# Shift added as rows: a two-block kernel's first k, v and queries projected from h without adaLN's shift

## The chip, the cores and the metric

One core of a Trainium2 chip runs the whole program. The metric is device time in microseconds (us) for one execution, the median of several runs; less is better. Everything is float32.

## What is computed

The input is x (256 tokens by 2048) and a context ctx of the same size. A first block of two layers (adaLN, one input projection, attention with pooling and Fourier branches, gates, an output projection) is followed by a second block (spatial gating, an LRU and an FFN). The change touches the first layer of the first block only:

```python
shift, scale, gate = jnp.split(jax.nn.silu(c) @ ada_w[l] + ada_b[l], 3, axis=-1)
h = rmsnorm(x, norm_g[l]) * (1.0 + scale[:, None]) + shift[:, None]
hc = rmsnorm(xc, norm_g[l]) * (1.0 + scale_c) + shift_c        # the context, with c_ctx
qc, kc, vc, upc, ufc, gc = split_proj(hc @ w_in[l])
q, k, v, up, uf, g = split_proj(h @ w_in[l])                   # 1024, 256, 256, 512, 512, 2048 columns
q = apply_axial_rope(rmsnorm(q.reshape(B, N, N_HEADS, HEAD_DIM), q_norm_g[l]), cos, sin)
k = apply_axial_rope(rmsnorm(k.reshape(B, N, N_KV_HEADS, HEAD_DIM), k_norm_g[l]), cos, sin)
att = latent_attention(q, k, v, kc, vc)
x_new = x + gate[:, None] * (jnp.concatenate([att, pool, fourier], -1) * silu(g)) @ w_out[l]
```

Here silu(c) @ ada_w[l] needs 2048 by 6144 weights (50 MB) for two vectors, the one of x and the one of the context.

## The kernel before

**Chunks.** All large weights come through one ring: the list `chunks` holds one entry per 512 KB of a weight matrix, SyncE loads them in order into RAW (NRAW = 8 buffers, `load_ahead`, L257, and L1071). A load is put once the chunk eight places before it is released: a chunk of the ada form when it is multiplied, another when it is split. There are two kinds of work on a chunk:
- ada chunks (256 rows of ada_w by 512 columns): TensorE (PE) multiplies them in plain float32 against the two vectors silu(c), silu(c_ctx) (L1104), 8 chunks to one of 12 groups of 512 columns per layer: groups 0 to 3 are the shift, 4 to 7 the scale, 8 to 11 the gate. Then ACT copies the sums out (`ada_out`, L1330), PE turns them (L1172), and DVE writes them as columns (L1576 to L1584); the last two steps are a popped step, `spread`.
- the others are split into two fp32r parts, high on ACT (L1320), low on DVE (L1546), in one of NSPL = 4 buffers, and multiplied three times. In layer 0 tokens and context go together ("wide": 24 matmuls of 128x512 per chunk). k and v (the `kv` group), q0 (heads 0 to 3), q1 (heads 4 to 7), the pool input gp, the Fourier input gf and the eight gate groups use L1123 to L1125 or L1137 to L1139. The output projection out0 has 8 groups of 4 chunks.

**One list sets the order.** The program is written once as a list `order` of steps; every engine runs its own instructions of each step in that order, waiting on semaphores. `run_chunks` (L307) goes through the chunks: `run_ahead` (L272) first puts the splits of the next chunks (those up to START_AHEAD = 3 places on while the position is under 72, AHEAD = 5 later), then small steps are popped from two queues, `hi` and, if that is empty, `low` (`pop_side`, L286: in layer 0 one step per half chunk; in the start two per two ada chunks), then the matmuls are put, then what the chunk triggers (`then`). `need` pops further steps until the h that a chunk reads has been put.

**The start of layer 0** (`start`, L707): for u = 0 to 3 eight ada chunks of scale group 4+u and eight of shift group u; from u = 1 on two kv chunks between them, after 12 and after 16 ada chunks; then the last two kv chunks. In `hi` stand the squares of x, the 16 turns of x into columns (`turn_x`, L1158 on PE, L1557 on DVE) and rstd (L979). The end of each u appends eight tiles of h (`tile_h`, L433: DVE L1590, ACT L1338, DVE L1595), and for u = 3 the loads of the rope tables, `tables` (L475, DVE L1606 and L1609, waits for the spill of x) and the DFT load. x is spilled from XT to memory (L1936), since XT is used again for QS, the rows of q, k and v.

**After it** come q0, q1, gp, gf and the gates, with two chunks of `left` (16 later ada groups, 128 chunks) after every two (`mixed`, L344), then out0 in the same manner (L942), eight ada chunks (FILL), and layer 1. At the end of a projection `rows_out` (L485; ACT L1356, DVE L1617) copies PSUM banks to QS; `norm_item` (L497) squares, scales, ropes and turns. Attention goes in units of one head and 128 queries; `unit_row` (L555) runs four stages of four units, scores (PE L1187), max, exp (ACT L1383), scaling, turns (L1194) and the product with v (L1204). There are 32 units in layer 0, heads 0 to 3 first in the list; `gate_out` (L644) of heads j0 and j0+1 pops until their units are put (the gate groups come in the order 8, 10, 0, 2, 4, 6, 12, 14). `x_out` (L692) at the end of an out0 group adds to x (DVE L1714) and puts two squares (ACT L1454).

## Time and profile before

| | |
|---|---|
| median of 3 runs | 2459.34 us (2458.92 to 2460.93) |
| the profiled execution | 2455.74 us, of which the profile's span is 2453.9 us |
| mean granted TensorE clock in it | 0.976 |
| PE busy | 2318.9 us, 94% |
| DVE, ACT, POOL busy | 1288.8, 1044.1, 196.6 us |
| memory read and written | 428.37 and 6.29 MB, 177 GB/s |

The engines are PE (TensorE), DVE (VectorE), ACT (ScalarE), POOL (GpSimd) and SP (SyncE). A matmul's record is longer than its spacing, since matmuls are pipelined, so costs of PE are read from starts. Where an engine stood idle, the profile says what ended the wait. Idle time of an engine that does not set the end costs nothing.

### The profile page before, as it was taken

The numbers are of one execution on the slowest core, as the hardware profiler recorded it, in microseconds if no ns is written. First come the engines' busy times: TensorE is split into PE (matmuls) and PEld (weight loads), VectorE is DVE, ScalarE is ACT, GpSimd is POOL, SyncE is SP. The second block draws the span as 40 slices with busy tenths as digits, with TensorE's granted clock in tenths as the row PEclk, the third lists the DMA queues.
The fourth block names the chain that finished last, engine by engine and source line by source line (L and its number), as shares of the span: only waits on it lengthen the run. The fifth ranks groups of instructions, "written<-read, shape, count | busy, mean of one in ns | idle before, by whom it ended". The sixth has DMA issues, their size and how long they took to land.

```text
span 2453.9 us, 30582 instructions
## 1 busy us (share of the span) xinstructions
PE 2318.9 (94%) x12135; PEld 1857.9 (76%) x12135; DVE 1288.8 (53%) x2110; ACT 1044.1 (43%) x1596; POOL 196.6 (8%) x237
## 2 busy tenths in 40 slices
PE   5889999999999997899998988989999999999998
PEld 2467777777777665678887877868888888888887
DVE  2444533132332254445666786556765666566664
ACT  2232333342321263445544555445543555345543
POOL 1000100000010122100012014120000000000001
PEclk8989999999999998999999999989999999999999
DMA  9764343435655583534555554545555555566652
GB/s 367 284 246 163 131 140 108 138 104 172 240 172 172 183 302 114 188 105 141 186 172 155 175 186 129 173 135 187 184 189 185 184 186 187 190 188 188 195 187 89
DMA packets 347021, 436.66 MB, mean 178 GB/s; under 512 B 13848, under 2 KB 269280, under 8 KB 345984
## 3 DMA queue, kind: packets, MB, share of 16 engines
q1 hardware_dynamic: 341376, 413.19, 51.1%
q0 software_dynamic: 3408, 16.38, 1.8%
q10 hardware_dynamic: 2096, 5.15, 0.6%
q8 instruction: 96, 1.57, 0.3%
q14 instruction: 45, 0.37, 0.0%
HBM read 428.37 MB, written 6.29 MB: 177 GB/s over the span
## 4 chain that ended last, share of the span: by engine, by line
PE 84%; DVE 5%; ACT 4%; DMA 3%; POOL 2%; issue 2%; SPq 0%; ACTq 0%; POOLq 0%; DVEq 0%
PE ps L1142 31%; PE ps L1143 16%; PE ps L1137 5%; PE ps L1139 5%; PE ps L1138 5%; PE ps L1123 4%; PE ps L1125 4%; PE ps L1124 4%; PE ps L1104 3%; ACT SPL L1320 2%; DMA RAW<-in_w_in_dram 2%; DVE SPL L1546 1%; PE ps L1187 1%; PE ps L1204 1%; DMA RAW<-in_ada_w_dram 1%
## 5 line engine op out<-in xcount | busy, mean ns | idle before, releaser
L1142 PE MATMUL ps<-HS,SPL 128*128 128x512 f32 x3456 | 1230.0, 401 | 18.0 <-POOL HS L1998 17.0
L1546 DVE TENSOR_TENSOR SPL<-RAW,SPL 128x1024 fp32r<-128x1024 f32 x592 | 725.7, 1231 | 667.2 <-ACT SPL L1320 665.6
L1143 PE MATMUL ps<-HS,SPL 128*128 128x256 f32 x3456 | 968.8, 280 | 0.0
L1320 ACT ACTIVATE SPL<-RAW 128x1024 fp32r<-128x1024 f32 x592 | 621.8, 1057 | 538.1 <-PE ps L1143 349.6
L1142 PEld LDWEIGHTS ps<-HS,SPL 128*128 128x128 f32 x3456 | 654.3, 189 | 182.3 <-POOL HS L1998 17.6
L1143 PEld LDWEIGHTS ps<-HS,SPL 128*128 128x128 f32 x3456 | 656.6, 190 | 2.1 <-issue 1.9
L1123 PE MATMUL ps<-SPL,HS 128*128 128x512 f32 x576 | 248.0, 430 | 22.3 <-ACT XT L1362 8.6
L1125 PE MATMUL ps<-SPL,HS 128*128 128x512 f32 x576 | 228.3, 396 | 0.0
L1124 PE MATMUL ps<-SPL,HS 128*128 128x512 f32 x576 | 228.1, 396 | 0.0
L1137 PE MATMUL ps<-HS,SPL 128*128 128x512 f32 x512 | 212.3, 415 | 1.2 <-DVE HS L1702 1.2
L1139 PE MATMUL ps<-HS,SPL 128*128 128x512 f32 x512 | 200.5, 392 | 0.0
L1138 PE MATMUL ps<-HS,SPL 128*128 128x512 f32 x512 | 200.1, 391 | 0.0
L1123 PEld LDWEIGHTS ps<-SPL,HS 128*128 128x128 f32 x576 | 110.5, 192 | 72.8 <-issue 20.8
L1993 POOL TENSOR_TENSOR TMP<-TMP 128x256 f32<-128x256 f32 (+1 forms) x68 | 61.6, 906 | 1235.2 <-ACT TMP L1454 1232.7
L1124 PEld LDWEIGHTS ps<-SPL,HS 128*128 128x128 f32 x576 | 110.6, 192 | 26.7 <-issue 6.0
L1137 PEld LDWEIGHTS ps<-HS,SPL 128*128 128x128 f32 x512 | 96.6, 189 | 43.8 <-issue 16.1
L1125 PEld LDWEIGHTS ps<-SPL,HS 128*128 128x128 f32 x576 | 110.1, 191 | 24.8
L1104 PE MATMUL ps<-RAW,CW 128*32 128x512 f32 x768 | 114.5, 631 | 11.4 <-DMA RAW<-in_ada_w_dram 9.3
L1454 ACT ACTIVATE TMP<-XT 128x256 f32<-128x256 f32 (+1 forms) x72 | 33.5, 465 | 191.9 <-DVE XT L1714 124.1
L1138 PEld LDWEIGHTS ps<-HS,SPL 128*128 128x128 f32 x512 | 96.7, 189 | 22.4 <-issue 3.8
L1139 PEld LDWEIGHTS ps<-HS,SPL 128*128 128x128 f32 x512 | 96.4, 188 | 21.1
L1899 DVE SCALAR_TENSOR_TENSOR MM<-MM,VV 128x256 f32<-128x256 f32 x192 | 80.0, 478 | 0.0
(251 smaller groups left out, 1542.0 us busy)
## 6 DMA issues: line engine op xcount, KB each, us to landing
RAW<-in_w_in_dram SPq DMA_DIRECT2D x208, 512.0 KB, 5.7
RAW<-in_ada_w_dram SPq DMA_DIRECT2D x192, 512.0 KB, 4.9
RAW<-in_ffn_w_up_dram SPq DMA_DIRECT2D x192, 512.0 KB, 3.5
RAW<-in_w_out_dram SPq DMA_DIRECT2D x96, 512.0 KB, 4.5
RAW<-in_ffn_w_down_dram SPq DMA_DIRECT2D x96, 512.0 KB, 3.3
x_spill<-XT POOLq DMA_DIRECT2D x2, 2048.0 KB, 15.1
XT<-x_spill POOLq DMA_DIRECT2D x1, 4096.0 KB, 16.1
MM<-in_x_dram ACTq DMA_DIRECT2D x2, 1024.0 KB, 10.6
```

What stands on the lines that cost most here:

```text
L1104: m = mm(PS[6][32 * q:32 * q + 32, :], CW[:, 2 * k:2 * k + 32], raw_of(i)[:, kk * 512:(kk + 1) * 512], start=kc < 2, stop=kc >= 6, skip_gr ...
L1123: mm(PS[b][:, :], hr, wr, start=k == 0, stop=False, skip_group_check=True)
L1124: mm(PS[b][:, :], hr, wl, start=False, stop=False, skip_group_check=True)
L1125: m = mm(PS[b][:, :], hl, wr, start=False, stop=k == KT - 1, skip_group_check=True)
L1137: mm(PS[b][:, :], wr, hr, start=k == 0, stop=False, skip_group_check=True)
L1138: mm(PS[b][:, :], wr, hl, start=False, stop=False, skip_group_check=True)
L1139: m = mm(PS[b][:, :], wl, hr, start=False, stop=k == KT - 1, skip_group_check=True)
L1142: mm(PS[b][:, :], wr, hh, start=k == 0, stop=False, skip_group_check=True)
L1143: m = mm(PS[b][:, 256:512], wl, hh[:, 0:256], start=False, stop=k == KT - 1, skip_group_check=True)
L1320: act(SPL[:, (n - 1) % NSPL, 0, :], raw_of(i), ACT.Copy).then_inc(s_hi, 1)
L1546: tt(w[:, 1, :], raw_of(s["i"]), w[:, 0, :].bitcast(F32), ALU.subtract).then_inc(s_lo, 1)
L1899: stt(o, CV[c][:, tap:tap + 256], V(c_fw[tap] + col), o, ALU.mult, ALU.add).then_inc(s_ct, 1)
```

## The change

For k, v and the queries of heads 0 to 3 in layer 0, the product is now (h without shift) @ W plus a row, shift @ W, that is the same for all tokens. Only the scale is needed ahead of them. Concretely:
- `start(u)` runs eight ada chunks of scale group 4+u only, with kv chunks after 4 and 8 of them; six steps are popped per two ada chunks in u = 0. h is made without shift.
- `go_on(u)` then runs shift group u (8 ada chunks) and two q0 chunks, which read the same h; behind them `shift_h` makes h again with shift (32 tiles: DVE sum, ACT copy, DVE subtraction).
- k, v and q0 leave PSUM to BARE, in MM, instead of QS. Their 16 w_in chunks are loaded a second time, in the ada form (`shift_rows`), four after every two chunks of q1, with the shift's columns as the vectors. The sum is spread over 128 partitions by two matmuls (tokens, context), DVE adds it to the rows, and the norms follow. The list of units takes heads 0 to 3 after that.
- q0's and q1's share of `left` moves: out0 now has four ada chunks after every two of its own, layer 1 eight beside its projections instead of 24.

The diff, cut to its core:

```diff
-            while at["taken"] < min(len(queue), at["pos"] + (START_AHEAD if at["pos"] < 72 else at["ahead"])):
+            while at["taken"] < min(len(queue), at["pos"] + (START_AHEAD if at["pos"] < 80 else at["ahead"])):
...
-                    pop_side(2 if c.group.side == 2 and c.kc % 2 == 0 else 0)
+                    pop_side(c.group.side if c.kc % 2 == 0 else 0)
...
-        def mixed(main, left):
+        def mixed(main, left, per=2):
             seq = []
-            for c in main:
-                seq.append(c)
-                if len(seq) % 4 == 2:
-                    seq.extend(left[:2])
-                    del left[:2]
+            for i in range(0, len(main), 2):
+                seq.extend(main[i:i + 2] + left[:per])
+                del left[:per]
...
+        def shift_h(k, s, bare, done, used):
+
+            y = {}
+
+            def s0():
+                y["slot"], last = take()
+                y["h"] = put("h0", l=0, k=k, s=s, slot=y["slot"], shifted=True, last=[ada_ready[0, k // 4], bare[k, s], *last])["n"]
+
+            def s1():
+                y["h"] = put("h1", l=0, k=k, s=s, slot=y["slot"], scaled=y["h"], last=[used])["n"]
+
+            def s2():
+                h = put("h2", l=0, k=k, s=s, slot=y["slot"], hi=y["h"], again=0)
+                give(y["slot"], (s_h2, h["n"]))
+                done[k, s] = (s_h2, h["n"])
+            return [s0, s1, s2]
+
         def layer(l):
...
+            def bare_out(which):
+                def f():
+                    x["bare"][which] = copy_rows([0, 1, 2, 3], 512, [BARE[which][:, i, :] for i in range(4)], [multiplied()])
+                return f
+
+            def shift_rows(which):
+
+                def after():
+                    slot, last = take()
+                    s = put("ada_out", slot=slot, last=[multiplied(), *last])
+                    bank_last[6] = [(s_adaE, s["n"])]
+                    if not hi:
+                        hi.append(idle)
+                    hi.insert(1, lambda: add(slot, s["n"]))
+
+                def add(slot, out):
+                    while "scr_a" not in x:
+                        hi.pop(0)()
+                    s = put("shift_rows", which=which, slot=slot, out=out, ready=x["bare"][which], last=x["scr_a"], after=use(4, 5))
+                    n = 4 * s["n"]
+                    give(slot, (s_sp, s["n"]))
+                    bank_last[4], bank_last[5] = [(s_srow, n)], [(s_srow, n)]
+                    if which == 0:
+                        hi.extend(staged([norm_item(i, 2, 1, tt, (s_srow, n - 3 + i), lv.KTr[:, :, i * 128:(i + 1) * 128], BARE[0][:, i, 0:256])
+                                          for i, tt in enumerate(TILES)]))
+                    else:
+                        hi.extend(staged([norm_item(i, 4, 0, tt, (s_srow, n - 3 + i), MV[:, tt[0], 0:4, tt[1] * 128:(tt[1] + 1) * 128], BARE[1][:, i, :])
+                                          for i, tt in enumerate(TILES)]) + [lambda: start_units(0)])
+                return group("ada", "shift", W, (1024, 0)[which], [6], after)
 
             def kv_out():
...
-            kv = group("tm", ("kv", l), W, 1024, [0, 1, 2, 3], kv_out, TILES)
-            q0 = group("tm", ("in", l), W, 0, qb[0], q_out(0, qb[0]), lv.tiles)
+            kv = group("tm", ("kv", l), W, 1024, [0, 1, 2, 3], bare_out(0) if both else kv_out, TILES)
+            q0 = group("tm", ("kv", l), W, 0, qb[0], bare_out(1), TILES) if both else group("tm", ("in", l), W, 0, qb[0], q_out(0, qb[0]), lv.tiles)
...
-                cs = ada_group(0, 4 + u, 2) + ada_group(0, u, 2)
+                cs = ada_group(0, 4 + u, 2 if u else 6)
                 after_ada = cs[-1].then
 
                 def start_h():
                     after_ada()
                     if u == 3:
                         put("spill", last=[multiplied()])
-                    hi.extend(staged([tile_h(0, k, s, x, h) for k in range(4 * u, 4 * u + 4) for s in range(2)])
-                              + ([load_tables, tables, load_dft] if u == 3 else []))
+                    hi.extend(staged([tile_h(0, k, s, x, bare) for k in range(4 * u, 4 * u + 4) for s in range(2)])
+                              + ([lambda: put("select_in"), load_tables, tables, load_dft] if u == 3 else []))
                 cs[-1].then = start_h
-                return cs[:12] + kv[2 * u - 2:2 * u - 1] + cs[12:] + kv[2 * u - 1:2 * u] if u else cs
+                return cs[:4] + kv[2 * u - 2:2 * u - 1] + cs[4:] + kv[2 * u - 1:2 * u] if u else cs
+
+            def go_on(u):
+
+                c = q0[2 * u + 1]
+                after_q = c.then
+
+                def add_shift():
+                    while (0, u) not in ada_ready:
+                        hi.pop(0)()
+                    used = multiplied()
+                    hi.extend(staged([shift_h(k, s, bare, h, used) for k in range(4 * u, 4 * u + 4) for s in range(2)]))
+                    if after_q:
+                        after_q()
+                c.then = add_shift
+                return ada_group(0, u, 2) + q0[2 * u:2 * u + 2]
 
...
-                main = [c for u in range(4) for c in start(u)] + kv[6:8], q0 + q1 + gp + gf + gates
+                main = ([c for u in range(4) for c in start(u)] + kv[6:8] + [c for u in range(4) for c in go_on(u)]
+                        + mixed(q1, shift_rows(0) + shift_rows(1), 4)), gp + gf + gates
...
-        lay_out(mixed(outs0, left))
+        lay_out(mixed(outs0, left, 4))
...
+                elif kind == "shift_rows":
+                    for sm, v in new((s_sel, 16)):
+                        e.wait_ge(sm, v)
+                    e.wait_ge(s_adaE, s["out"])
+                    for src in range(2):
+                        m = mm(PS[4 + src][:, :], SPREAD[:, src, :], T(s["slot"]), start=True, stop=True, skip_group_check=True)
+                    m.then_inc(s_sp, 1)
+
...
+                    if s["shifted"]:
+                        stt(T(s["slot"])[:, 0:256], HX(0, k, src, 0).bitcast(F32), shift(0, k, src), HX(0, k, src, 1).bitcast(F32), ALU.add, ALU.add).then_inc(s_h0, 1)
+                        continue
...
+                elif kind == "shift_rows":
+                    rows = BARE[s["which"]]
+                    for sm, v in new(*s["last"], *s["ready"]):
+                        e.wait_ge(sm, v)
+                    e.wait_ge(s_sp, n)
+                    for i in range(4):
+                        part = PS[4 + i // 2]
+                        if s["which"] == 0:
+                            tt(lay[0].VT[:, i, :], rows[:, i, 256:512], part[:, 256:512], ALU.add).then_inc(s_v, 1)
+                            tt(rows[:, i, 0:256], rows[:, i, 0:256], part[:, 0:256], ALU.add).then_inc(s_srow, 1)
+                        else:
+                            tt(rows[:, i, :], rows[:, i, :], part[:, :], ALU.add).then_inc(s_srow, 1)
 
                 elif kind == "tables":
...
+                elif kind == "select_in":
+                    for sm, v in new((s_xt, KT), (s_sqx, 4)):
+                        e.wait_ge(sm, v)
+                    e.dma_start(SPREAD, I["k_spread"]).then_inc(s_sel, 16)
```

## Rows read from the trace of the kernel before

**Rows 1.** The page's 40 slices of 61 us, PE, busy tenths

```profile
PE   5889999999999997899998988989999999999998
```

**Rows 2.** Windows; columns as in their first line

```profile
core 0: us, PE busy (x) PEld busy (x) DVE busy (x) ACT busy (x) POOL busy (x), PEclk, DMA share, GB/s
10.00:66.00 56.00, 37.84 (x202) 15.03 (x202) 17.21 (x41) 13.36 (x17) 1.04 (x1) 0.82 0.95 352
66.00:161.00 95.00, 74.96 (x358) 45.72 (x359) 39.30 (x93) 29.24 (x52) 1.94 (x3) 0.91 0.89 319
161.00:848.00 687.00, 682.45 (x3230) 511.38 (x3228) 233.92 (x413) 198.84 (x309) 38.92 (x39) 0.99 0.45 153
861.00:918.00 57.00, 55.55 (x256) 38.15 (x256) 32.02 (x53) 36.74 (x59) 16.13 (x21) 0.97 0.86 298
```

**Rows 3.** Timeline of PE, start: start, duration, line, idle time before

```profile
53.42 0.66 PE L1158 MATMUL ps<-IDN,MM 128*128 128x128 f32 x4
...
66.28 0.47 PE L1123 MATMUL ps<-SPL,HS 128*128 128x512 f32 x1 [0.65 <-DVE HS L1595]
...
67.85 0.47 PE L1123 MATMUL ps<-SPL,HS 128*128 128x512 f32 x1 [0.64 <-DVE HS L1595]
...
74.67 0.50 PE L1123 MATMUL ps<-SPL,HS 128*128 128x512 f32 x1
...
80.82 3.81 PE L1104 MATMUL ps<-RAW,CW 128*32 128x512 f32 x32
...
93.88 0.80 PE L1123 MATMUL ps<-SPL,HS 128*128 128x512 f32 x1 [2.65 <-DVE SPL L1546]
...
160.33 0.76 PE L1123 MATMUL ps<-SPL,HS 128*128 128x512 f32 x1 [8.28 <-ACT XT L1362]
```

**Rows 4.** Timeline of ACT and DVE, 20 to 70 us

```profile
23.72 1.91 ACT L1325 ACTIVATE HS<-MM 128x2048 fp32r<-128x2048 f32 x1 [1.27 <-DMA MM<-in_ctx_dram]
...
48.70 1.29 DVE L1557 COPY XT<-ps 128x512 f32<-128x512 f32 x2 [1.42 <-PE ps L1158]
...
57.57 1.23 DVE L1546 TENSOR_TENSOR SPL<-RAW,SPL 128x1024 fp32r<-128x1024 f32 x1 [4.74 <-ACT SPL L1320]
58.72 0.68 DVE L1557 COPY XT<-ps 128x512 f32<-128x512 f32 x1
...
63.80 0.87 DVE L1590 SCALAR_TENSOR_TENSOR TMP<-XT,S,ps 128x256 f32<-128x256 f32 x2 [2.23 <-PE ps L1165]
```

**Rows 5.** Timeline of POOL, ACT's queue and DVE, 130 to 160 us

```profile
133.30 1.18 POOL L1936 DMA_DIRECT2D x_spill<-XT  x2 [72.63 <-PE ps L1104]
...
146.45 0.53 ACTq L1349 DMA_DIRECT2D GX<-in_k_norm_g_dram  x1
...
156.93 0.43 DVE L1606 TENSOR_TENSOR XT<-TMP,GX 128x256 f32<-128x256 f32 x1 [10.49 <-DMA GX<-in_k_norm_g_dram]
```

**Rows 6.** The page's groups of instructions, splits: busy, mean ns, idle before

```profile
L1546 DVE TENSOR_TENSOR SPL<-RAW,SPL 128x1024 fp32r<-128x1024 f32 x592 | 725.7, 1231 | 667.2 <-ACT SPL L1320 665.6
...
L1320 ACT ACTIVATE SPL<-RAW 128x1024 fp32r<-128x1024 f32 x592 | 621.8, 1057 | 538.1 <-PE ps L1143 349.6
```

**Rows 7.** Timeline of ACT, rows out at the end of q0

```profile
210.84 1.08 ACT L1356 ACTIVATE XT<-ps 128x512 f32<-128x512 f32 x2 [10.98 <-PE ps L1125]
```

**Rows 8.** Timeline of PE and ACT, attention units among q1's neighbours

```profile
302.79 1.16 PE L1204 MATMUL ps<-XT 128*128 128x128 f32 x8
...
304.01 1.02 PE L1187 MATMUL ps<-XT,MM 128*128 128x512 f32 x2
...
306.57 0.19 ACT L1383 ACTIVATION_READ_ACCUMULATOR XT<-ps,SM 128x1 f32 x1
...
312.81 0.60 PE L1187 MATMUL ps<-XT,MM 128*128 128x256 f32 x2
...
314.98 0.19 ACT L1383 ACTIVATION_READ_ACCUMULATOR XT<-ps,SM 128x1 f32 x1
```

**Rows 9.** Timeline of DVE and ACT, the last group end of out0

```profile
848.10 1.66 DVE L1714 SCALAR_TENSOR_TENSOR XT<-ps,ADA,XT 128x256 f32<-128x256 f32 x4 [17.63 <-PE ps L1139]
...
849.79 0.63 ACT L1454 ACTIVATE TMP<-XT 128x512 f32<-128x512 f32 x1 [0.15 <-DVE XT L1714]
```

More of the change, by code:

```diff
@@ L357, in two_block_program, with need_shift @@
         ada_ready, s2_ready = {}, {}
+        need["ada"] = lambda k: [(s_c, 1)]
+        def need_shift(k):
+            while any((0, g) not in ada_ready for g in range(4)):
+                hi.pop(0)()
+            return [ada_ready[0, g] for g in range(4)]
+        need["shift"] = need_shift
         def ada_group(l, g, side=0):
@@ L464, in need_x @@
                 return [h[k, 0]]
-            need["kv", l] = need_both
+            need["kv", l] = need_bare if both else need_both
             need["in", l] = need_both if both else need_x
@@ L485, in rows_out, with copy_rows @@
             def rows_out(banks, width):
-                if both or x.get("qs_used"):
+                if x.get("qs_used"):
                     flush(hi)
                 x["qs_used"] = True
-                s = put("rows_out", l=l, banks=banks, width=width, last=[multiplied(), *x["qs"]], a=count.get("qa", 0), d=count.get("qd", 0))
-                x["qs"] = []
+                while "tab" not in x:
+                    hi.pop(0)()
+                last, x["qs"] = [multiplied(), *x["qs"]], []
+                return copy_rows(banks, width, [lv.QS[:, i, 0:width] for i in range(len(banks))], last)
+            def copy_rows(banks, width, dest, last):
+                put("rows_out", banks=banks, width=width, dest=dest, last=last)
                 ready = []
@@ L502, in s0 @@
                     slot, last = take()
-                    s = put("n0", l=l, i=i, nh=nh, slot=slot, last=[ready, *last])
+                    s = put("n0", l=l, i=i, nh=nh, rows=xq, slot=slot, last=[ready, *last])
                     give(slot, (s_nred, s["n"]))
@@ L507, in s1 @@
                     (a, last), (c, more) = (take(), take()) if rope else ((None, []), (None, []))
-                    s = put("n1", l=l, i=i, nh=nh, which=which, t=tt[1], rope=rope, a=a, c=c, last=last + more + [x["tables"]], rope_n=tick("rope") if rope else 0)
+                    s = put("n1", l=l, i=i, nh=nh, rows=xq, which=which, t=tt[1], rope=rope, a=a, c=c, last=last + more + [x["tables"]], rope_n=tick("rope") if rope else 0)
                     if rope:
```

73 lines of the change are left out of this document (43 added, 30 removed).

## The prediction, made before the changed kernel ran

> **What bounds the kernel now.** The page's 40 slices come first [rows 1]: PE is near 9 tenths nearly everywhere but in the first slices of 61 us. The windows view splits the run [rows 2]: from 10 to 66 us PE is busy 37.8 of 56 us with DMA at 0.95; from 66 to 161, 75.0 of 95 with DMA at 0.89; from 161 to 848, 682.5 of 687. After 161 us a new wait is paid in full and new PE work too. The change adds PE work, so its whole gain must come out of the 38 us of PE idle time before 161.
>
> The PE timeline shows where that idle time is [rows 3]. The first k, v chunk starts at 66.28. It needs h, and h needs all of x turned into columns, rstd, and scale and shift of group 0; by the order of the list it also stands behind 28 ada chunks. The DVE and ACT rows give that chain [rows 4]: the last tile of x lands at 23.72, its turns follow two at a time between ada chunks, and the last turned tile is copied only at 58.72. Two later waits are of another kind: 2.65 us at 93.88 for the split of a w_in chunk, and 8.28 us until 160.33, since k and v cannot leave PSUM before the spill and the rope tables: spill issued at 133.30, the last table load at 146.45, DVE idle 10.49 us on it [rows 5].
>
> **Prices.** An ada chunk costs PE 3.81/8 = 0.48 us; a wide chunk is kv1's, 80.82 − 74.67, less 0.6 for the ada turn in it: 5.5 us [rows 3]. A load of 0.524 MB at 352/0.95 = 370 GB/s takes 1.4 us [rows 2]. A split is 1.06 on ACT, then 1.23 on DVE [rows 6].
>
> **Part 1, the earlier start.** Removed ahead of the first kv chunk: 16 of 28 ada chunks; and six steps are popped per two ada chunks instead of two, so the turns run together. x still lands at 23.7. Sixteen copies at 1.29/2 = 0.65 us put the start of the last at 34.5; from there the first h took 63.80 − 58.72 = 5.1 [rows 4], the spread of group 4 and the first split, now behind rstd, add 2.1: 41.7. From the first h to kv1's start took 74.67 − 63.80 = 10.9, four ada chunks in it: kv0 ends at 50.4 with a clock as today, against 72.4. From there to kv7's end PE has 7 wide chunks (38.5), 20 ada chunks (9.6) and turns (1). Also h is late: after an ada group its turn stands in the middle of the next kv chunk, whose other half is 2.7 us, while the four tiles that come first need 67.85 − 63.80 = 4.1 plus a split, 5.3 to 5.5. With 1.9 us of ada between, that is 1.0 late twice; before kv6 nothing stands between, 2.8; I take 7 in all for these and for splits that queue among them. kv7 ends at 106.5. Loads are not late: 40 chunks and x are 25 MB, 68 us.
>
> **Part 2, the second shift.** k and v now go to MM and wait for neither spill nor tables. But `tables` stands on DVE right behind, at go_on(0)'s first chunks, ahead of q0's first split. Its loads leave at 106.5; the spill, issued near 87, is nearly done, so I take 6 us rather than 10.45 [rows 5], plus 1.8 for the tables themselves and 1.2 for the split: q0 starts at 115.5, 5 us after its eight ada chunks. Then come four rounds of 8 ada and 2 wide chunks, 14.8 us each. q0's chunk i is loaded once chunk i−8, the round's first ada chunk, is multiplied: 3.5 us to land, 2.4 to split, against 3.8 of ada, 2.1 late in three rounds. The first matmul after the 2.65 us of idle took 0.80 us against 0.50 at 74.67, and the mean granted clock of 66 to 161 was 0.91, so some 17 of its 95 us ran at 1.2 instead of 2.4 GHz [rows 2, 3]; for such falls I add 3. q0 ends at 115.5 + 11 + 3 x 14.8 + 6.3 + 3 = 180; today 210.8 [rows 7]. **Lead 31 us**; bounds 23 (tables 10.5, h 10) and 39 (no wait for tables, none for loads, no fall).
>
> **Part 3, what is owed.** By 210.8 today's kernel has also done 6 later ada chunks (2.9 us) and k's turns (1.1). New: 16 chunks of the ada form for the shift's rows, 7.7; four 128x512 spreads at about 0.9 (a pair of such records took 1.02 [rows 8]), 3.6. Together **15.3**. The 32 new DVE sums, 32 ACT copies and 32 subtractions, near 0.45 us each (0.87 for two [rows 4]), cost nothing: DVE is busy 39 of 95 us, ACT 29 [rows 2]; without that cover they would be 1.3 us a tile on PE's path. The extra 8.4 MB of loads, 23 us, lie beside q1, where PE has 44 us of its own and DMA stands at 0.45. v's copies move from ACT to DVE, both idle then. The one new load (select rows, tiny) is on POOL behind the spill, ahead of the dft load, which needs the spill anyway: nothing.
>
> **Part 4, new waits**, all where PE is full. (a) q1 follows q0 at once in the same banks: two DVE copies, 1.4. (b) AHEAD looks 5 chunks ahead. With four ada chunks between pairs the next main chunk is number +5, one too far: its split is put only after whatever the pair's last chunk triggers. At q1's end that is rows_out (1.08), then the split 2.3 and 0.2: 3.6 against 1.9 of ada, 1.8. (c) The same at the 7 inner group ends of out0 (32 chunks, now four ada per pair), where x_out and two squares are put first. The last group end of today shows that chain [rows 9]: x_out starts at 848.10, the second square ends at 849.79 + 0.63 = 850.42. Behind it ACT's 1.06, DVE's 1.23 and 0.1: 852.8, 4.8 us after the matmuls, of which four ada chunks cover 1.9. 2.85 x 7 = **20**; bounds 14 and 27. For falls of the clock behind them I take 3. The trace shows DVE in order: the copy at 58.72, whose turn stood at 53.42, came after the split at 57.57 that waited for ACT [rows 3, 4]. The Trainium skill (TensorE: Matmul & The Clock Gate, section Architectural detail: the array is 16× 32×32, not 1× 128×128) says so of ScalarE and VectorE both, strict FIFO, while TensorE may pull weight loads ahead; by that rule the split cannot pass the squares, and without it the 20 would be 0.
> (d) Attention. The units of heads 0 to 3 can start only after shift_rows(1), that is behind heads 4 to 7 in the list. gate_out(0) needs heads 0 and 1, 27 unit rows. Counted in the code, 56 steps are popped from gp's first chunk to gate 0's end; 41 go to norms, pool, fourier and ada spreads, 15 are unit rows, 12 are forced with no weight matmul between. A 512 row runs 304.01 to 306.76 from scores to exp, a 256 row 312.81 to 315.17 [rows 8], 2.5 with the latter's slack off, of which PE's own is 2.2 (302.79 to 305.03) or half of it, 1.7: 0.8 x 12 = **10**, bounds 5 and 15.
> (e) Less ada in layer 1 (8 chunks instead of 24 beside the projections; 861 to 918 has 1.45 us of idle at DMA 0.86 [rows 2]): −1.5.
>
> **Sum:** −31 + 15.3 + 1.4 + 1.8 + 20 + 3 + 10 − 1.5 = **+19**. The profiled execution took 2455.7, 3.6 below the median of the runs: 2475 on its scale, 2478 on the median's, which I give. Ends: −39 + 15.3 + 3.2 + 14 + 5 − 1.5 = −3, and −23 + 15.3 + 3.2 + 27 + 3 + 15 = +40.
>
> **Rivals.**
> 1. *Faster: out0 has no gaps.* If the next chunk's split is not held by x_out and the squares, 23 fall away: 2455; with the lead at 39, 2447. It decides at 0.55 us per group end with a lead of 31, at 1.7 with 39. For it: today's out0 hides the same chain. Against: today two ada chunks stand there and the next two main chunks are in reach of 5. Chance 0.17.
> 2. *The start hardly moves.* Rstd, x's columns and h are one chain after 23.7, and h is late at every group. With kv7's end at 125 the lead is 12: 2497. Against: the turns were spaced by loads, not by DVE (1.42 us idle before each pair [rows 4]). Chance 0.10.
> 3. *The clock falls behind most new gaps.* A chunk at the lower level takes 11 instead of 5.5; a fall of half a chunk is 2.7 us. Five more in out0: +14, 2492. Against: these gaps stand in dense work. Chance 0.13.
> 4. *All shrinks together:* q1's 16 chunks eat the lead, gaps and attention are small: 2459. Chance 0.10.
> The forecast: 0.50.
>
> **Numbers.** 0.2% is 4.9 us, about what a measurement of this kernel can tell from no change. Rival 1 gives faster 0.12 and same 0.05; rival 4 same 0.06, faster 0.03; all else is slower: 0.15, 0.11, 0.74. The range runs from rival 1's better case to beyond rival 2, short of the worst sum: 2447 to 2501.
>
> **What would show it.** First h near 42, kv7's end near 106, q0's rows out near 180: parts 1 and 2. Seven PE gaps near 2.8 us in out0 released by DVE's split: 4c; under 0.6 each, the sign turns. A stretch of unit rows without weight matmuls near gate 0: 4d. PE idle in q1 with DMA full would say that the 16 loads were not hidden. The forecast is wrong altogether if q0 ends before 165 or out0 shows no gap.

## The result, and the profile after

| | before | after |
|---|---|---|
| median | 2459.36 us (2458.92 to 2460.93) | 2526.39 us (2520.10 to 2531.29) |
| ratio | | 1.0270, 95% interval 1.0247 to 1.0293 |
| the profiled execution, its span | 2455.74, 2453.9 | 2531.29, 2529.5 |
| mean granted clock in it | 0.976 | 0.969 |

The change makes the kernel 67 us slower, and the forecast (2478, at most 2501) is missed on the slow side. The page's busy shares of PE in 40 slices, now of 63 us each (compare [rows 1]):

```profile
PE   6889899989988886999998998989999999999998
```

The first slice rose from 5 to 6, but slices 5, 9 and 12 to 15 fell from 9 to 8: the end of q1, the middle of the gates, and out0. (Slices 16 and 17, 7 and 8 before, are 6 and 9 now.) The windows view of the kernel after says the same in us (columns as in [rows 2]):

```profile
10.00:45.00 35.00, 20.93 (x130) 11.83 (x131) 16.03 (x37) 12.01 (x15) 1.04 (x1) 1.00 0.87 304
45.00:119.00 74.00, 63.14 (x316) 40.43 (x316) 35.38 (x88) 24.32 (x44) 2.48 (x4) 0.94 0.89 328
119.00:195.00 76.00, 64.04 (x304) 45.07 (x304) 31.10 (x67) 18.62 (x36) 0.00 (x0) 0.90 0.71 255
195.00:695.00 500.00, 476.98 (x2247) 351.92 (x2248) 184.50 (x364) 158.26 (x266) 24.81 (x26) 0.98 0.42 145
695.00:920.00 225.00, 199.66 (x926) 144.31 (x925) 52.54 (x74) 40.26 (x49) 16.46 (x13) 0.92 0.58 196
```

PE idles 12 us while q0 is projected (119 to 195), 23 us from there to out0 and 25 us in out0, where it idled in none of 171 us before, and in q0 and out0 its granted clock falls to 0.90 and 0.92.

Read at four marks, the two profiled executions differ as follows. "Lead" is the time before minus the time after; the marks are rows of DVE and ACT (the rows out of q0 [rows 7], x_out of out0's first and last group [rows 9], the same row of layer 1's last output group, at 1277.94 and 1346.70).

| stretch | before | after | difference | forecast |
|---|---|---|---|---|
| to q0's rows out | 210.84 | 194.74 | −16.1 | −31 |
| to out0's first x_out | 466.4 | 500.7 | +34.3 | +20.8 |
| out0, first to last x_out | 170.9 | 224.9 | +54.0 | +38.4 |
| layer 1, to its last output group | 429.8 | 426.4 | −3.5 | −9.2 |
| the rest, whose code is the same | 1176.0 | 1182.8 | +6.8 | 0 |
| sum | | | +75.6 | +19 |

The forecast's column is its own sum, sorted by place. The 32 ada chunks that move into out0 stand there with 15.4 us, at 0.48 each; of these, 2.9 are taken out of the work owed, 4.8 off beside q1 and 7.7 off layer 1. The two profiled executions lie 75.6 us apart and the medians 67: the one after is the slowest of its four.

**The start.** The timeline of PE in the kernel after, first matmuls of k, v and of q0's four rounds (compare [rows 3]):

```profile
45.00 0.47 PE L1209 MATMUL ps<-SPL,HS 128*128 128x512 f32 x1 [2.15 <-DVE HS L1694]
...
119.82 0.77 PE L1209 MATMUL ps<-SPL,HS 128*128 128x512 f32 x1 [7.64 <-DVE SPL L1642]
...
140.66 0.50 PE L1209 MATMUL ps<-SPL,HS 128*128 128x512 f32 x1 [3.64 <-DVE SPL L1642]
...
161.06 0.50 PE L1209 MATMUL ps<-SPL,HS 128*128 128x512 f32 x1 [3.59 <-DVE SPL L1642]
...
181.47 0.50 PE L1209 MATMUL ps<-SPL,HS 128*128 128x512 f32 x1 [3.61 <-DVE SPL L1642]
```

k and v start 21 us earlier, and kv's last matmul starts at 105.86, as forecast (106.5). The wait of 7.64 us ahead of q0 holds DVE's own wait for the rope tables' last load, ahead of `tables` and of the split:

```profile
116.70 0.43 DVE L1718 TENSOR_TENSOR XT<-TMP,GX 128x256 f32<-128x256 f32 x1 [9.12 <-DMA GX<-in_k_norm_g_dram]
```

After it a round takes 20.4 us, of which 3.6 are the wait for the split. One round, all engines: L1190 are ada chunks, SPq the loads, L1414 and L1642 the split's two halves.

```profile
133.38 3.64 PE L1190 MATMUL ps<-RAW,CW 128*32 128x512 f32 x32
...
134.48 0.88 SPq L1156 DMA_DIRECT2D RAW<-in_w_in_dram  x2
...
138.29 1.06 ACT L1414 ACTIVATE SPL<-RAW 128x1024 fp32r<-128x1024 f32 x1 [1.56 <-DMA RAW<-in_w_in_dram]
...
139.38 1.22 DVE L1642 TENSOR_TENSOR SPL<-RAW,SPL 128x1024 fp32r<-128x1024 f32 x1 [2.37 <-ACT SPL L1414]
```

The load leaves 1.1 us after the round's first ada matmul, lands 3.8 later, and the split takes 2.4: 7.3 us against 3.64 of ada chunks, which leaves the 3.6 of waiting.

**Out0.** The end of its first group in the kernel after (compare [rows 9]):

```profile
695.36 1.92 PE L1190 MATMUL ps<-RAW,CW 128*32 128x512 f32 x16
695.47 1.66 DVE L1826 SCALAR_TENSOR_TENSOR XT<-ps,ADA,XT 128x256 f32<-128x256 f32 x4 [14.58 <-PE ps L1225]
...
697.16 0.63 ACT L1550 ACTIVATE TMP<-XT 128x512 f32<-128x512 f32 x1 [0.15 <-DVE XT L1826]
...
697.70 1.99 ACT L1414 ACTIVATE SPL<-RAW 128x1024 fp32r<-128x1024 f32 x2
...
698.77 2.59 DVE L1642 TENSOR_TENSOR SPL<-RAW,SPL 128x1024 fp32r<-128x1024 f32 x2 [1.64 <-ACT SPL L1414]
...
700.37 0.47 PE L1223 MATMUL ps<-HS,SPL 128*128 128x512 f32 x1 [3.09 <-DVE SPL L1642]
```

x_out, two squares, ACT's half, DVE's half, matmul: the forecast's chain, link by link, and seven times (the waits view of PE, 660 to 900, has one line over 1.2 us: engine, line, for what; us, times, longest):

```profile
PE ps L1223 <- DVE SPL L1642: 25.3, 7, 3.7
```

Behind each of these waits the matmuls come at wider spacing for a while. PE's timeline behind the first one, two neighbours soon after it and two a little later:

```profile
701.67 0.63 PE L1224 MATMUL ps<-HS,SPL 128*128 128x512 f32 x1
702.09 0.63 PE L1225 MATMUL ps<-HS,SPL 128*128 128x512 f32 x1
...
706.60 0.39 PE L1223 MATMUL ps<-HS,SPL 128*128 128x512 f32 x1
706.83 0.39 PE L1224 MATMUL ps<-HS,SPL 128*128 128x512 f32 x1
```

The starts are 0.42 us apart, then 0.23.

### The profile page after: what moved, and what is told of

The parts are those of the page before. It is cut to its first block, busy times and chain, and to the rows that moved or that the text cites. A ratio compares the mean times of both kernels' runs of the same rounds, so it can differ in the third digit from the quotient of the medians.

```text
span 2529.5 us, 30855 instructions
## 1 busy us (share of the span) xinstructions
PE 2348.4 (93%) x12207; PEld 1884.9 (75%) x12207; DVE 1318.1 (52%) x2186; ACT 1054.5 (42%) x1628; POOL 197.5 (8%) x238
## 4 chain that ended last, share of the span: by engine, by line
PE 84%; DVE 6%; ACT 4%; issue 2%; DMA 2%; POOL 1%; ACTq 0%; POOLq 0%; DVEq 0%
PE ps L1228 31%; PE ps L1229 16%; PE ps L1223 5%; PE ps L1225 5%; PE ps L1224 5%; PE ps L1209 4%; PE ps L1211 4%; PE ps L1210 4%; ACT SPL L1414 2%; PE ps L1190 2%; DVE SPL L1642 2%; PE ps L1281 1%; PE ps L1298 1%; PE ps L1324 1%; DMA RAW<-in_w_in_dram 1%
## 5 line engine op out<-in xcount | busy, mean ns | idle before, releaser
L1228 PE MATMUL ps<-HS,SPL 128*128 128x512 f32 x3456 | 1236.7, 402 | 17.1 <-POOL HS L2115 16.3
L1642 DVE TENSOR_TENSOR SPL<-RAW,SPL 128x1024 fp32r<-128x1024 f32 x592 | 725.9, 1233 | 608.4 <-ACT SPL L1414 606.5
L1414 ACT ACTIVATE SPL<-RAW 128x1024 fp32r<-128x1024 f32 x592 | 621.7, 1056 | 524.2 <-PE ps L1229 357.8
L1223 PE MATMUL ps<-HS,SPL 128*128 128x512 f32 x512 | 218.3, 426 | 26.5 <-DVE SPL L1642 25.3
L1225 PE MATMUL ps<-HS,SPL 128*128 128x512 f32 x512 | 205.8, 402 | 0.0
L1224 PE MATMUL ps<-HS,SPL 128*128 128x512 f32 x512 | 205.4, 401 | 0.0
L1209 PEld LDWEIGHTS ps<-SPL,HS 128*128 128x128 f32 x576 | 112.2, 195 | 80.2 <-issue 27.1
L1210 PEld LDWEIGHTS ps<-SPL,HS 128*128 128x128 f32 x576 | 112.6, 196 | 26.7 <-issue 5.3
L1211 PEld LDWEIGHTS ps<-SPL,HS 128*128 128x128 f32 x576 | 111.5, 194 | 25.2
L1826 DVE SCALAR_TENSOR_TENSOR XT<-ps,ADA,XT 128x256 f32<-128x256 f32 x64 | 28.0, 480 | 147.0 <-PE ps L1225 143.3
L1190 PE MATMUL ps<-RAW,CW 128*32 128x512 f32 x768 | 98.9, 610 | 4.3 <-DMA RAW<-in_ada_w_dram 2.3
```

What stands on the lines that cost most here:

```text
L1190: m = mm(PS[6][32 * q:32 * q + 32, :], vec, raw_of(i)[:, kk * 512:(kk + 1) * 512], start=kc < 2, stop=kc >= 6, skip_group_check=True)
L1209: mm(PS[b][:, :], hr, wr, start=k == 0, stop=False, skip_group_check=True)
L1210: mm(PS[b][:, :], hr, wl, start=False, stop=False, skip_group_check=True)
L1211: m = mm(PS[b][:, :], hl, wr, start=False, stop=k == KT - 1, skip_group_check=True)
L1223: mm(PS[b][:, :], wr, hr, start=k == 0, stop=False, skip_group_check=True)
L1224: mm(PS[b][:, :], wr, hl, start=False, stop=False, skip_group_check=True)
```

## The experiments

The runs of one comparison share the chip and its runs of the kernel before; the three comparisons had medians of 2457.9 (first four kernels), 2455.2 (second four) and 2460.3 us (last four) for it. Since the code behind layer 1 is the same everywhere and yet takes 1167 to 1189 us (last section), places are compared by their own marks, and the medians stand beside them.

### Out0: is it the place of the split in the list?

**out_ahead7**

```diff
+        at["ahead"] = 7
         end0 = add_up0(marks[1])
```

> The changed kernel, but in out0 the list looks 7 chunks ahead instead of 5, so the split of the next pair's first chunk is put ahead of x_out and the two squares, with the four ada chunks between pairs left as they are. Theory A (the split stands in its engines' queues behind x_out and the squares, so the matmuls of the next group wait): the seven waits of 3.1 to 3.7 us for DVE's split at the inner group ends fall below 0.6 us; from the first to the last x_out it takes 224.8 less 25 and less up to 13 for the clock, 187 to 200 us; the whole 2526 less 25 to 38, 2488 to 2501 us. Theory B (the split is late because its chunk lands late, or because DVE is slowed while POOL sums): looking ahead changes little, each wait stays above 2 us, the whole 2520 to 2530 us.

Measured: 2481.7 us (2474.2 to 2491.8), ratio 1.0094 (1.0061 to 1.0128). The same place in the profile of this kernel:

```profile
693.63 1.23 DVE L1643 TENSOR_TENSOR SPL<-RAW,SPL 128x1024 fp32r<-128x1024 f32 x1 [12.58 <-ACT SPL L1415]
...
695.09 1.23 DVE L1643 TENSOR_TENSOR SPL<-RAW,SPL 128x1024 fp32r<-128x1024 f32 x1 [0.23 <-ACT SPL L1415]
695.55 1.92 PE L1191 MATMUL ps<-RAW,CW 128*32 128x512 f32 x16
696.23 1.65 DVE L1827 SCALAR_TENSOR_TENSOR XT<-ps,ADA,XT 128x256 f32<-128x256 f32 x4
```

Both splits now stand ahead of x_out, no wait for a split is left, and from 700 to 850 PE is busy 150.00 of 150 us at clock 1.00 (134.79 and 0.92 in the kernel after). Out0 takes 184.2 us, 40.6 less: the waits' 25.3 and 15.3 more. Those 15.3 are matmuls at the lower clock: behind each wait they follow at 0.43 us instead of 0.23, for 2.2 us on average beyond the wait itself. Counted directly in the kernel after, the starts behind the seven waits that are more than 0.26 us apart add up to 16 us over the usual 0.227, 1.8 to 2.9 behind each. Theory A holds; the 13.4 us that are left above the 170.9 of before are the 32 moved ada chunks, 0.42 each.

**out_ahead6**

```diff
+        at["ahead"] = 6
         end0 = add_up0(marks[1])
```

> The changed kernel with a look-ahead of 6 in out0 instead of 5 (7 was measured). Theory A (with four ada chunks between pairs the next split is one position too far for 5, and nothing else is wrong): 6 does what 7 did, no wait for DVE's split at group ends, first to last x_out 184 us, the whole 2475 to 2492 us. Rival (the split needs its full time ahead, and 6 puts it only one chunk of 5.4 us before the group end): waits of 1 to 2 us stay, first to last x_out 192 to 205 us.

Measured: 2478.5 and 2487.5 us; out0 184.8 us, no wait for a split. One place decides, as counted.

**out_two**

```diff
-        lay_out(mixed(outs0, left, 4))
+        seq = []
+        for i in range(0, 32, 4):
+            seq += outs0[i:i + 2] + left[:3] + outs0[i + 2:i + 4] + left[3:5]
+            del left[:5]
+        lay_out(seq)
```

> The changed kernel, but out0 gets only two ada chunks at each group end and three in the middle of a group (40 instead of 64; the 24 others go beside layer 1's projections). Theory A (four ada chunks put the next split out of reach of the look-ahead of 5): no wait above 0.6 us at group ends; first to last x_out falls from 224.8 to before's 170.9 plus 8 ada chunks of 0.48, some 175 us, and layer 1 takes 5 to 12 us more for its 24 further ada chunks: 2526 - 50 + 5 to 12 = 2481 to 2488 us. Theory B (the waits come from the engines themselves, which are as busy with two chunks as with four): the waits stay near 3 us, the gaps' 25 us with them, and only the moved 11.5 us of PE work leave out0 and come back in layer 1: 2515 to 2526 us.

Measured: 2488.9 us (2480.5 to 2490.9), ratio 1.0124 (1.0100 to 1.0148). Out0 takes 182.2 us, not 175: the splits' waits are gone, but PE now waits 3.4 us, in three places, for ACT's copy of an ada group's sums, and some 2 us of slow matmuls follow. Layer 1 takes 433.1 instead of 426.4, 6.8 us for 24 chunks: 0.28 each, against 0.42 in out0. Theory A again for the cause, but short of its 175 and just outside its 2481 to 2488 us, for the most part by these new small waits.

**before_out_four**

```diff
-        lay_out(mixed(outs0, left))
+        four = left[:56]
+        del left[:56]
+        lay_out(mixed(outs0, four, 4))
```

> The kernel before, with one part of the change alone: four ada chunks after each of the first 14 pairs of out0 instead of two after all 16 (56 instead of 32; 24 fewer beside layer 1). Theory A (this placement alone makes the loss of out0, whatever the start does): seven waits of 3 to 3.7 us released by DVE's split, 25 us, plus 24 x 0.48 = 11.5 of moved PE work, plus 0 to 13 of lower clock: out0 from 170.9 to 207 to 220 us; layer 1 gives back 4 to 10; the whole 2459 + 26 to 45 = 2485 to 2504 us. Rival (the loss in out0 is a follow-up of the changed start): out0 grows by the 11.5 alone and layer 1 gives them back: 2457 to 2465 us.

Measured: 2504.5 us (2491.8 to 2507.8), ratio 1.0175 (1.0142 to 1.0208). In the waits view of this kernel, PE, 660 to 900 us:

```profile
PE ps L1137 <- DVE SPL L1546: 25.3, 7, 3.7
```

Seven waits of the same 25.3 us in a kernel whose start is not touched: out0 takes 223.1 us, above the expected 220, since the slow matmuls cost some 15 again, and layer 1 gives back 10.4. So this placement costs 42 us by its marks (52.2 in out0 less 10.4) and 43 by the ratio, of the 67. It is shown both ways, added to the kernel before and, as the late split alone, taken out of the kernel after (40.6).

### The gates: the order of heads

**gates_order**

```diff
-GATES = (8, 10, 0, 2, 4, 6, 12, 14), (8, 10, 12, 14, 0, 2, 4, 6)
+GATES = (8, 10, 4, 6, 0, 2, 12, 14), (8, 10, 12, 14, 0, 2, 4, 6)
```

> The changed kernel with one constant changed: layer 0's gate groups run in the order 8, 10, 4, 6, 0, 2, 12, 14 instead of 8, 10, 0, 2, 4, 6, 12, 14, since the attention units of heads 4 to 7 now stand ahead of those of heads 0 to 3. Theory A (the rows forced at gate 0 are work that is owed anyway, and only their idle time of about 1 us each, two waits of 2.1 us at the gate steps and some slow matmuls behind are lost): no stretch of unit rows without weight matmuls at 501 to 533 us; the kernel gains 12 to 18 us: 2508 to 2514 us. Rival (the whole 35 us by which the lead shrinks from the gate of groups 10 to that of 2 are waits): 2486 to 2496 us. Second rival (what the forced stretch loses would be lost in the gates' stage in another way, because ACT and DVE are the bound there): 2522 to 2530 us.

Measured: 2514.0 us (2512.7 to 2517.6), ratio 1.0225 (1.0204 to 1.0246). Windows of the kernel after, and of this one:

```profile
501.00:533.00 32.00, 23.23 (x126) 16.24 (x128) 17.82 (x60) 15.77 (x37) 0.00 (x0) 0.95 0.00 1
```

```profile
500.00:535.00 35.00, 35.00 (x192) 27.66 (x185) 17.57 (x46) 14.45 (x29) 0.00 (x0) 1.00 0.38 121
```

DMA at 0.00 marks the forced stretch: no weight chunk is freed, since attention units run alone, and PE idles 8.8 of 32 us. With the heads that come first also gated first, it is full, and out0's first x_out moves from 695.5 to 681.7: 13.8 us. The whole gains 12 us by the medians, as theory A has it. That the rest of the fall of the lead between these gates is work that was owed is argued from this, not shown by a run of its own.

### The start: which part made it early, and why the rounds are slow

**after_pop2**

```diff
-                cs = ada_group(0, 4 + u, 2 if u else 6)
+                cs = ada_group(0, 4 + u, 2)
```

> The changed kernel, but two steps are popped per two ada chunks of the first group, as in the kernel before, instead of six: x's turns are spread out again, the 16 ada chunks stay removed. Theory A (x's turns in one run and the removed ada chunks are both needed for the early start; with two steps per pair the turns fall behind the few chunks that are left and are popped in one burst by the first k, v chunk's need): first k, v matmul at 48 to 55 us instead of 45.0, the whole 3 to 8 us slower than the changed kernel, 2529 to 2534 us. Theory B (the pops decide nothing, since the list forces what is needed): first k, v matmul within 2 us of 45.0, the whole within its own spread, 2520 to 2530 us.

Measured: 2531.4 and 2536.5 us; first k, v matmul at 50.99, out0's last x_out 5.1 us later. Theory A; in only two runs, so it rests on the marks.

**before_pop6**

```diff
-                cs = ada_group(0, 4 + u, 2) + ada_group(0, u, 2)
+                cs = ada_group(0, 4 + u, 2 if u else 6) + ada_group(0, u, 2)
...
-                    pop_side(2 if c.group.side == 2 and c.kc % 2 == 0 else 0)
+                    pop_side(c.group.side if c.group.side > 1 and c.kc % 2 == 0 else 0)
```

> The kernel before with one part of the change alone: six steps popped per two ada chunks of the first group instead of two. Theory A (first k, v stands behind 28 ada chunks whose loads, with x, are 19 MB at 370 GB/s, 52 us): the turns are done near 35, but the first k, v matmul moves only from 66.3 to 53 to 58 us, and most of that is lost again in front of the spill's and the tables' loads, which keep q0 near 155: the whole 2 to 6 us faster than the kernel before. Rival (the late turns were the whole delay, and the first layer's start can be had without its second h): first k, v near 48 and the whole 10 us or more faster. Second rival: no change within 2 us.

Measured: 2459.5 us (2451.0 to 2467.6), ratio 0.9997 (0.9984 to 1.0010): nothing. The turns were done near 35 us, but k, v start at 64.44. PE's timeline between, an ada chunk per row:

```profile
51.19 1.05 PE L1104 MATMUL ps<-RAW,CW 128*32 128x512 f32 x4 [0.29 <-DMA RAW<-in_ada_w_dram]
52.56 1.05 PE L1104 MATMUL ps<-RAW,CW 128*32 128x512 f32 x4 [0.32 <-DMA RAW<-in_ada_w_dram]
53.92 1.05 PE L1104 MATMUL ps<-RAW,CW 128*32 128x512 f32 x4 [0.30 <-DMA RAW<-in_ada_w_dram]
```

One chunk per 1.36 us: the ada chunks arrive no faster (0.524 MB in it, 385 GB/s), and the first kv chunk stands behind 28 of them. Theory A missed the place (53 to 58) by 6 us or more and its gain of 2 to 6 us; the second rival, no change within 2 us, holds. So of the 21.3 us by which k and v start earlier in the kernel after, taking back the quicker turns costs 6.0, and the other 15.3 come from the second h (fewer ada chunks ahead). Without the second h the quicker turns give only 1.8 us at this place.

**q0_inter**

```diff
-                return ada_group(0, u, 2) + q0[2 * u:2 * u + 2]
+                cs = ada_group(0, u, 2)
+                return cs[:4] + q0[2 * u:2 * u + 1] + cs[4:] + q0[2 * u + 1:2 * u + 2]
```

> The changed kernel, but in each round of go_on the list holds four ada chunks, a q0 chunk, four ada chunks, a q0 chunk, instead of eight ada and two q0 chunks. Theory A (a round's 3.6 us of waiting is the landing of its first q0 chunk, whose buffer comes free only with the round's first ada chunk): the waits for DVE's split in rounds 2 to 4 fall below 1 us, a round takes 15 to 17 us instead of 20.4 and the rows of q0 go out near 180 to 185 instead of 194.7; the whole 2526 less 9 to 15: 2511 to 2517 us. Theory B (the split waits behind ada turns and h's second steps in the list): the waits stay, or become two of half the size; q0's rows go out after 191, the whole 2520 to 2530 us.

Measured: 2514.2 us (2508.6 to 2519.8), ratio 1.0246 (1.0210 to 1.0282). The waits of rounds 2 to 4 are 0.92 us each, a round takes 16.5, q0's rows go out at 183.2. Theory A, though the first q0 chunk waits longer (12.10 us, until 118.02), since fewer ada chunks stand ahead of it.

**tables_late**

```diff
-                              + ([lambda: put("select_in"), load_tables, tables, load_dft] if u == 3 else []))
+                              + ([lambda: put("select_in"), load_tables] if u == 3 else []))
...
-                    hi.extend(staged([shift_h(k, s, bare, h, used) for k in range(4 * u, 4 * u + 4) for s in range(2)]))
+                    hi.extend(([tables, load_dft] if u == 0 else []) + staged([shift_h(k, s, bare, h, used) for k in range(4 * u, 4 * u + 4) for s in range(2)]))
```

> The changed kernel, but the rope tables' computation and the load behind it stand after q0's first two chunks instead of before them. Theory A (the 7.6 us of waiting ahead of q0's first matmul at 119.82 is DVE standing at the tables' loads, with the split behind it): q0 starts near 112, and q0's rows go out 6 to 9 us earlier: 2526 less 6 to 9, 2517 to 2520 us. Theory B (the first q0 chunk itself lands late, behind the loads and spills of that time): q0 still starts after 117 and the whole stays at 2522 to 2530 us.

Measured: 2520.5 us (2519.0 to 2527.3), ratio 1.0270 (1.0238 to 1.0302). q0 starts at 116.68, between the two theories; its rows go out only 2.4 us earlier. The profile of this kernel:

```profile
105.18 0.88 SPq L1156 DMA_DIRECT2D RAW<-in_w_in_dram  x2
...
114.22 1.06 ACT L1414 ACTIVATE SPL<-RAW 128x1024 fp32r<-128x1024 f32 x1 [8.94 <-DMA RAW<-in_w_in_dram]
115.31 2.51 DVE L1642 TENSOR_TENSOR SPL<-RAW,SPL 128x1024 fp32r<-128x1024 f32 x2 [9.82 <-ACT SPL L1414]
...
116.68 0.77 PE L1209 MATMUL ps<-SPL,HS 128*128 128x512 f32 x1 [4.20 <-DVE SPL L1642]
```

The tables no longer hold DVE; the chunk itself, issued when the group's first ada chunk is done, lands 9 us later, with other loads under way. Two waits lay on top of each other, the tables' and the landing: in q0_inter's profile ACT has done its half of the first q0 chunk's split at 106.7, and DVE stands 9.50 us at the tables' loads, while here the chunk itself is late, and with both edits together (four_edits below) it starts at 108.26. The first k, v matmul stands 1 us earlier in these two profiles than in the kernel after, so the 2.4 us here are partly that.

### Together

**four_edits** is out_ahead7, gates_order, q0_inter and tables_late in one kernel.

> Four edits together on the changed kernel: look-ahead 7 in out0, gate order 8, 10, 4, 6, 0, 2, 12, 14, the rounds of q0 with their ada chunks in two halves, the tables after q0's first chunks. If the four losses are apart and add up: 2526 - 44 (measured alone) - 12 (measured alone) - 9 to 15 - 6 to 9 = 2446 to 2455 us, a little below the kernel before (2458). If the start's gain is taken back by the transfers beside q1 (16 loads of the shift's rows): 2460 to 2470 us, with PE waiting for loads between 180 and 250.

Measured: 2450.2 us (2444.6 to 2458.1, 10 runs), ratio 0.9982 (0.9963 to 1.0001). q0 starts at 108.26 and its rows go out at 171.4, 23.4 us earlier than in the kernel after, more than the 11.5 and 2.4 of the two edits alone: the overlaid waits go together. (Five_edits below has the same code up to there and 173.6, so such a mark is good to some 2 us.) At layer 1's last output group it stands at 1267.8, against 1277.9 before and 1346.7 after: 78.9 us, of them 23.4 to q0's rows out, 13.8 for the gates by the run alone, 40.4 in out0, with 1.3 left over. The losses of the three places are apart and add up.

**all_edits** adds out_two's placement, `side=0` for the chunks of the shift's rows (they pop no steps), and `START_AHEAD if at["pos"] < 40`.

> The four edits and three more: only 40 ada chunks in out0 (two and three per pair, 24 more beside layer 1, where the chunks of the last comparison cost nearly nothing), the short look-ahead of 3 ends with the k, v chunks, and the 16 chunks of the shift's rows pop no steps of their own. Expected below four_edits: out0 from 184.2 to 175 us (9), of which layer 1 takes 0 to 5; the wait of 7.25 us at q1's end for a norm turn goes (5 to 8 with its clock); together 8 to 15 less than four_edits: 2435 to 2445 us. Rival (layer 1's chunks cost their full 0.48 us each and the norm steps are late in another place): within 4 us of four_edits.

Measured: 2447.5 us (2442.5 to 2456.6, 10 runs), ratio 0.9972 (0.9953 to 0.9991), within 3 us of four_edits as its rival has it. What it gains from q0's rows to out0, 6.4 us, is lost in the start, where q0's second chunk waits 4.24 us at 121.29 and q0's rows go out at 177.1 instead of 171.4. Nor does out_two's placement give what was expected of it: out0 takes 183.7 us, not 175, against 184.5 in four_edits, and layer 1 takes 4.0 more. Which of the three edits makes the wait at 121.29, this run alone can't tell. Five_edits has `side=0` and only 0.32 us there, and out_two's own run has q0's rows at 194.86 as in the kernel after, so the shorter START_AHEAD is left by elimination; it was not run alone.

**five_edits** is four_edits and `side=0` alone.

```diff
-                return group("ada", "shift", W, (1024, 0)[which], [6], after)
+                return group("ada", "shift", W, (1024, 0)[which], [6], after, side=0)
```

> The four edits of before (look-ahead 7 in out0, gate order, q0's rounds in halves, tables late) and a fifth: the 16 chunks of the shift's rows pop no steps of their own, so the norms of q1 are spread beside the later chunks. Expected: the wait of 7.25 us near 237 for the turn of a normed row goes, 5 to 9 us with its slow matmuls, and q0's rows go out at 171 as in four_edits: the end of layer 1 moves from 1267.8 to 1259 to 1263, the whole 2442 to 2447 us, 8 to 14 us below the kernel before. Rival (the norm steps that are pushed back are late for the first attention units, forced at a gate instead): layer 1 ends within 2 us of 1267.8.

Measured: 2442.5 us (2436.5 to 2446.3, 6 runs), ratio **0.9922** (0.9904 to 0.9940): 0.8% faster than the kernel before, and faster than the kernel after. At layer 1's last output group it stands at 1262.2, 15.8 us ahead of the kernel before and 5.7 ahead of four_edits, within the expected 1259 to 1263; the medians of the two, from different comparisons, lie 7.7 us apart. What it removes stands in the timeline of the kernel after, at q1's end:

```profile
259.56 0.69 DVE L1745 TENSOR_TENSOR XT<-XT,SM 128x512 f32<-128x512 f32 x1 [0.90 <-POOL SM L2078]
...
262.52 1.08 PE L1273 MATMUL ps<-IDN,XT 128*128 128x128 f32 x4 [7.25 <-DVE XT L1759]
```

The norms of q1's rows were popped between four shift chunks of 0.5 us each, and PE stood at the turn of the first. In five_edits the longest wait from 173 to 837 us is 1.7 us; from q1's first matmul to out0's first x_out it takes 477.2 us, against 484.2 in four_edits. Windows of five_edits, q0 and out0:

```profile
110.00:173.00 63.00, 61.49 (x319) 40.98 (x320) 32.03 (x76) 20.99 (x37) 0.00 (x0) 0.97 0.94 333
...
653.00:837.00 184.00, 184.00 (x924) 133.63 (x920) 45.55 (x73) 39.85 (x47) 16.75 (x13) 1.00 0.70 240
```

## Why the prediction was wrong, step by step

The sign was right, and the mechanisms named are there, but for one that is missing; the sum was 57 us short (75.6 against 19). The steps that failed are three: the term for the clock in out0 (3 us, it was 15.3), the end of q0 (a lead of 31 us, it was 16.1, by rounds of 20.4 instead of 14.8), and a term that the sum did not have, the norms' steps between the shift's chunks (some 7 to 10 us). They make 37 of the 57. By its steps:

- **Part 1 held.** kv7's end 106.2 against 106.5; k, v's start 21 us earlier. That removed ada chunks and quicker turns do this together is shown by the two runs on the pops.
- **Part 2 failed: the rounds of 14.8 us.** q0's end came at 194.7, not 180. 4.3 of it is the start of q0, 119.8 for 115.5. The price of the tables' loads was lowered from some 10 to 6 us on the ground that the spill was done; DVE stood 9.1 us, and 1.3 of copying k's and v's rows on DVE came before that and was not counted. Why the loads took so long was not tested; weight loads were under way at the time. 10.4 is the rounds: the 2.1 late (3.5 to land, 2.4 to split, against 3.8) was 3.6, since another 1.1 passes before the load leaves; and slow matmuls, for which 3 were added in all, cost some 2 us in every round (20.4 less 3.6 of ada, 3.6 of wait and 11 of wide chunks). Only with these waits all but removed (four_edits: one of 0.92 us is left) does q0 come to 63.1 us, near the forecast's 64.5, which had allowed 6.3 for waits and 3 for slow matmuls.
- **Part 3 held by its parts**: 0.48 us per chunk by its record (32 of them add 0.42 each to out0), loads hidden beside q1 (PE waits for none there), the second h hidden. But the steps popped between the 16 chunks were not looked at, only their matmuls: 7.25 us at q1's end and 2.4 at k's turns. That is the step that is missing from part 4, some 7 us with its clock by five_edits for q1's end and the turns together; without 4d, this stretch is 9.7 us above its forecast.
- **4a** 1.64 for 1.4. **4b** did not appear as such; the wait at that place is the norm's.
- **4c was right and too small.** 25.3 against 20, within 14 to 27: 3.1 us at the first group end and 3.7 at the others instead of 2.85. At the others DVE's two splits take 3.22 us instead of 2.59, beside two sums on POOL instead of one; two splits with no sum beside them take 2.35, as at 802.01:

```profile
728.19 2.67 POOL L2110 TENSOR_TENSOR TMP<-TMP 128x512 f32<-128x512 f32 x2 [29.05 <-ACT TMP L1550]
...
729.87 3.22 DVE L1642 TENSOR_TENSOR SPL<-RAW,SPL 128x1024 fp32r<-128x1024 f32 x2 [1.64 <-ACT SPL L1414]
...
732.10 0.76 PE L1223 MATMUL ps<-HS,SPL 128*128 128x512 f32 x1 [3.72 <-DVE SPL L1642]
...
802.01 2.35 DVE L1642 TENSOR_TENSOR SPL<-RAW,SPL 128x1024 fp32r<-128x1024 f32 x2
```

  The Trainium skill (GPSIMD Engine Reference, section 1. Specifications) says that GpSimd shares its SBUF interfaces with VectorE and contends with its instructions of two SBUF inputs, which the splits are; the trace agrees (3.22, 2.59 and 2.35 us beside two sums, one and none), though no run here takes the sum away. Of the Trainium skill's in-order rule that the prediction cited, out_ahead6 and out_ahead7 are the test: a split put ahead of x_out runs ahead of it, and one put behind waits.
- **The clock in out0 was the largest miss**: 15.3 for 3. The reason given against rival 3, "these gaps stand in dense work", is refuted: 2.2 us on average behind each of the seven waits, on dense work. Rival 3 named this mechanism and priced it at 14 us more in out0 (measured 12.3 more), with a chance of 0.13; its time, 2492, was still short, since q0's rounds and the norms were missing from it too.
- **4d** 13.8 against 10, bounds 5 to 15. In the forced stretch PE idles 8.8 us, 0.9 to 1.1 at each scores row and 2.1 once for DVE at a gate; of the other 5 of the 13.8, the granted clock of 0.95 there accounts for some 1.6, and the rest stays open.
- **4e and the moved chunks**: 7.7 + 1.5 were to come back in layer 1, 3.5 did. The runs price a chunk there at 0.22 (24 against 8, before and after) to 0.28 us (out_two), half of what it costs in out0: perhaps since beside projections that wait for h it partly fills holes, which no run tests. before_out_four, with all 24 taken away, gives 0.43, so the price is no constant.
- The last 6.8 us stand in code that is the same; next section.

The range failed on the terms' ends: it took each mechanism's bounds one by one, but none for what three of them share, the slow matmuls behind every wait. It also had no room beyond its own worst sum: +40 (40.5, or 39 with the −1.5 that it leaves out) is 2499 us on the medians' scale, so 2501 is not "short of the worst sum" but just past it. One figure is misread without effect: the wait for the tables is 10.49 us [rows 5], not 10.45.

## What to carry to other kernels

In a list that fixes every engine's order, chunks inserted between main chunks also use up the look-ahead in places: count from the last chunk of a group to the next split, and if it falls outside, the work at the group's end stands ahead of it on every engine that both use (here 5 against 6 places made 40 us). Price a wait on a full TensorE with the matmuls behind it (here 3.6 us of waiting cost 5.8), and bound that for all waits together. When one edit of two gives little, look for a second wait beneath the first before calling it hidden.

## What was not expected of the hardware

The same code ran at two rates while the granted clock read 1.00 in both. In the kernel before, the FFN's down projection, one group after another, DVE's first addition of each, in two places:

```profile
1877.53 0.42 DVE L1883 TENSOR_TENSOR XT<-ps,XT 128x256 f32<-128x256 f32 x1 [0.45 <-PE ps L1143]
...
1888.84 0.42 DVE L1883 TENSOR_TENSOR XT<-ps,XT 128x256 f32<-128x256 f32 x1 [0.45 <-PE ps L1143]
...
2103.83 0.42 DVE L1883 TENSOR_TENSOR XT<-ps,XT 128x256 f32<-128x256 f32 x1 [0.40 <-PE ps L1143]
...
2114.92 0.42 DVE L1883 TENSOR_TENSOR XT<-ps,XT 128x256 f32<-128x256 f32 x1 [0.40 <-PE ps L1143]
```

11.31 us a group, then 11.09, 1.9% less, with PE full in both (202.85 of 203 us and 199.67 of 200). The switch falls in another place from one profiled execution to the next, and gates_order shows only the slower rate in these projections. The part behind layer 1 takes 1167 to 1189 us in the fourteen profiles, and most of that spread lies in the stretch with these full projections, where 1.9% of some 800 us is 15 us; a lower granted clock in the stages ahead of them makes some of the rest (before_pop6, 1189 us, has 0.88 in the first 100 us behind layer 1, where the kernel before has 0.91). That is the size of the spread between runs of one kernel here (2 to 18 us over four runs or more), and the 6.8 us between the two profiles behind layer 1 lie within it. The cause of the two rates is not known from these traces.
